# First norm of a two-layer diffusion block: row tiles are loaded first, scaled by the root and turned, then modulated by feature in four units

## The chip, the cores and the metric

The kernel runs on one core of a Trainium2 chip. The metric is the time of one execution on the device in microseconds, median of several runs. The program is written out by hand for each engine: TensorE (PE), VectorE (DVE), ScalarE (ACT), GpSimd (POOL) and SyncE (SP), which issues most of the transfers. The engines meet through semaphores alone.

## What is computed

Two layers work on 512 latent rows and 256 context rows of 1024 features. A layer norms its input and modulates it with a shift and a scale that come from a conditioning vector (one for the latent rows, another for the context rows), multiplies by an input projection, runs two kinds of attention, merges them, and goes on to a gated convolutional channel mixer, normed and modulated the same way. The change touches only the first norm and what feeds it. Cut to that:

```python
def rms_norm(x, g):
    xf = x.astype(jnp.float32)
    y = xf * lax.rsqrt(jnp.mean(xf * xf, axis=-1, keepdims=True) + EPS)
    return (y * g.astype(jnp.float32)).astype(x.dtype)

def modulate(x, g, shift, scale):
    return rms_norm(x, g) * (1 + scale) + shift

sc, scc = jax.nn.silu(c), jax.nn.silu(c_ctx)
# layer 0; ada_w is 1024 x 6144
mod_lat = jnp.split(sc @ ada_w[0] + ada_b[0], 6, axis=-1)
mod_ctx = jnp.split(scc @ ada_w[0] + ada_b[0], 6, axis=-1)
h_lat = modulate(x, pre_mix_g[0], mod_lat[0], mod_lat[1])
h_ctx = modulate(ctx, pre_mix_g[0], mod_ctx[0], mod_ctx[1])
p_lat, p_ctx = h_lat @ even_w_in[0], h_ctx @ even_w_in[0]   # 1024 x 1184
```

## The kernel before

The rows are six tiles of 128 (`NT` = 6, of which `LT` = 4 latent), the features eight chunks of 128 (`KC` = 8). Every large product is made of three matmuls, high by high, high by low and low by high (lines 888 to 890), so each activation and each weight is split: ScalarE writes the high part (`act_hi`, `w_hi`), VectorE subtracts it from the full value (`act_lo`, `w_lo`; line 1897).

The start has three stages. First the *wide* products: `silu(c)` for both streams times the first 2048 columns of `ada_w` (shift and scale), in four units of 512 columns (`wide_mm`, line 914), each unit loaded in two halves of 1 MB by SP (`wide_unit`, line 751). VectorE adds the bias (line 2390). Two matmuls per unit with the selector `sel` spread each result row over the 128 partitions (`wide_spread`, line 925); ScalarE copies the shifts out (line 1871), VectorE makes 1 + scale times gain (line 2397). Then the norm of each row tile: load (line 661), square on ScalarE (line 1525), root on GpSimd (lines 2438 and 2440), scale (line 1982) and shift (line 1987) on VectorE over 1024 features, eight transposes on TensorE (line 945), high part and low part out of PSUM (lines 1543 and 1897). Behind each tile's transposes TensorE makes the last tile's first half of chunk 0 of the input projection (`first_tile`: 416 columns, features 0 to 511, weight unit 0). When all six are through, it makes the second half with weight unit 1.

Then come chunks 1 (512 columns, units 2 and 3) and 2 (256 columns, units 4 and 5). Woven in by the table `ADA_AT` are the *early* products, the other 16 units of 256 columns of `ada_w` (`ada_mm`, line 903), on PSUM banks 6 and 7 in turn: `ring_free(r)` makes TensorE wait until round r - 2 has been read out. The first two stand behind the last tile of chunk 0, the third behind tile 1 of unit 2:

```python
ADA_AT = {(1, 5): [0, 1], (2, 1): [2], (2, 3): [3], (2, 5): [4], (3, 1): [5], (3, 3): [6], (3, 5): [7],
```

VectorE reads them out in `early_evac` (line 1910, four additions), which it reaches in program order only after the six tiles of chunk 0. For each of those six, ScalarE squares two parts (line 1634) and copies the tile (line 1642), GpSimd makes two roots (lines 2438, 2440), VectorE scales by them (line 2097), and GpSimd issues a store (line 2516). ScalarE may be at most two tiles ahead of GpSimd. Ahead of tile 0 ScalarE splits weight unit 2 (line 1509) and VectorE makes its low part. Constants for later are loaded from ScalarE's queue, three behind each row tile (line 1557), and VectorE waits for all of them (`const_in`) ahead of its split of unit 2.

Of the kernel before, what the change touches and what calls it, by code (L numbers as in the profile page):

```python
# [29 lines left out]
WIDES = 2 * D // WIDE  # L30
TZ_W = 2 * GRID_W - 1
# [126 lines left out]
def build(nc, I, C, out):  # L158
# [16 lines left out]
    with ctx:  # L175
# [19 lines left out]
        cvec, cexp = sb("cvec", [P, KC, 2]), sb("cexp", [P, KC, 2])  # L195
# [26 lines left out]
        def kilo(n):  # L222
# [5 lines left out]
        wide_row = arena[:, 8 * D:10 * D]  # L228
        wide_raw = [arena[:, 14 * D + n * KC * WIDE:14 * D + (n + 1) * KC * WIDE].rearrange("p (k c) -> p k c", k=KC)
                    for n in range(2)]  # L230
        wide_raw += [nc.alloc_sbuf_tensor_at(f"wide_raw{n}", [P, KC, WIDE], fp32, offset=act_at + n * 4 * KC * ROWS)
                     for n in range(2)]
        sel = sb("sel", [P, 2, P])
# [50 lines left out]
        pe_raw, x_first = pt[1][1], pt[1][0]  # L284
# [25 lines left out]
        wide_clear, wide_bias, ident_in = sem("wide_clear"), sem("wide_bias"), sem("ident_in")  # L310
        spread, shift_out = sem("spread"), sem("shift_out")
# [48 lines left out]
        CVEC = [(cvec[:, :, :], C["streams"])]  # L360
        FIRST = [(ident[:, :], C["ident"]), (sel[:, :, :], C["sel"])]
# [19 lines left out]
        def norm_growth(tiles, y, h, streams):  # L381
            return dict(t=2 * tiles * h, th=2 * tiles * h, y=tiles * y, h=tiles * h, xl=tiles, xs=tiles * y,
                        mod=streams * (y + 2 * h), gain=y + h, nm=1)
# [4 lines left out]
            ("ada", dict(t=WIDES)),  # L388
            ("norm0", dict(norm_growth(NT, 0, 1, 2), mod=0)),
# [16 lines left out]
        BASE, total = {}, dict.fromkeys("t th mm w ev st s tt pv hd y h xl xs mod gain nm nsq f g".split(), 0)  # L406
# [74 lines left out]
        def ada_round(layer, g):  # L481

            if layer == 0:
                return base("in0", "t") + ADA_IN0[g - ADA_FIRST]
            return base("up0", "t") + g

# [90 lines left out]
        def _(sp):  # L577
# [67 lines left out]
            def x_moves(name, tiles):  # L645
# [3 lines left out]
                for t in tiles:  # L649
# [3 lines left out]
                    if t >= 2 and NORMS[name][0] is None:  # L653
                        sp.wait_ge(h_scaled, base(name, "h") + t - 1)
                    elif t >= 2:
# [16 lines left out]
            def head_loads(name, a, before, weights=()):  # L672
# [26 lines left out]
                def load(p, s):  # L699
# [4 lines left out]
                    if a.name == "mla":  # L704
                        pe_q = x_first if p == 0 else x_raw[s].rearrange("p (t c) -> p t c", t=NT)
# [41 lines left out]
            def wide_unit(n):  # L747

                v = I["ada_w"][0].rearrange("(k p) c -> p k c", p=P)[:, :, n * WIDE:(n + 1) * WIDE]
                for half, (a, b) in enumerate(((0, KC // 2), (KC // 2, KC))):  # L750
                    sp.dma_start(wide_raw[n][:, a:b, :], v[:, a:b, :]).then_inc(wide_in[n][half], 16)

            wide_unit(0)
            sp.wait_ge(wide_clear, 1)
            sp.dma_start(wide_row[0:2, :], I["ada_b"][0:1, 0:2 * D].to_broadcast([2, 2 * D])).then_inc(wide_bias, 16)
            for n in range(1, WIDES - 1):
                wide_unit(n)
            gain_loads("norm0")
            wide_unit(WIDES - 1)
            x_moves("norm0", range(2))  # L760
            for n in range(2):
                k_unit(n, I["even_w_in"][0], 4 * n, 4, 0, MLA_IN)
            x_moves("norm0", range(2, NT))
# [5 lines left out]
            sp.wait_ge(t_free, WIDES)  # L769
# [4 lines left out]
            sp.wait_ge(h_ready, base("norm0", "h") + NT)  # L774
# [108 lines left out]
        def _(pe):  # L883
# [23 lines left out]
            def wide_mm(n):  # L907

                ring_free(n)
                for k in range(KC):  # L910
                    c = k % GROUPS * GROUP
                    if k % (KC // 2) == 0:
                        pe.wait_ge(wide_in[n][k // (KC // 2)], 16)
                    last = mm(bank(6 + n % 2, WIDE)[c:c + GROUP, :], silu[:, k, :], wide_raw[n][:, k, :],
# [3 lines left out]
            def wide_spread(n):  # L918

                pe.wait_ge(t_free, n + 1)  # L920
# [1746 lines left out]
```

## Time and profile before

| what | value |
|---|---|
| median of 3 runs | 1719.76 us (1718.31 to 1721.81) |
| profiled execution, its own time | 1721.04 us |
| profiled execution, span | 1719.3 us |
| PE busy | 1656.8 us, 96% |
| DVE busy | 1005.9 us, 59% |
| ACT busy | 624.3 us, 36% |
| POOL busy | 259.6 us, 15% |
| DMA | 211.34 MB, mean 123 GB/s |

The own time is the device time of the profiled execution; the span runs from its first to its last recorded instruction. Busy shares are means over stages with different limits: in the first 21 us the transfers are full and TensorE has pauses, later TensorE is nearly always busy. Matmuls overlap and their ends are modelled, so the distance from start to start is the better measure of one.

### The profile page before, as it was taken

To read this page: it belongs to the slowest core of one execution; us is meant where nothing else is said; L and a number is where in the kernel's file an instruction comes from. 1 tells how busy PE (TensorE), PEld (TensorE's weight loads), DVE (VectorE), ACT (ScalarE), POOL (GpSimd) and SP (SyncE) were. 2 spreads that over 40 slices of the span, in tenths; PEclk is the share of its full clock that TensorE was granted. 3 is DMA by queue.
4 is the path that set the end of the run, shared out by engine and by line. 5 is a ranking of instruction groups with operands and counts; after the bars stand their busy time and mean duration, and the time that the engine had idled before them with its cause. 6 is when DMAs were issued, how large, how long until landed. Compare 5 with 4: busy or idle time off the path is not lost.

```text
span 1719.3 us, 26521 instructions
## 1 busy us (share of the span) xinstructions
PE 1656.8 (96%) x9828; PEld 1334.2 (78%) x9828; DVE 1005.9 (59%) x1911; ACT 624.3 (36%) x1077; POOL 259.6 (15%) x420
## 2 busy tenths in 40 slices
PE   6999899999999999999999989998999999999998
PEld 2877566668898888888878878886678888888886
DVE  3666566764747777767776487215753744443445
ACT  3414555653321212121324434225543433323343
POOL 1413233331300000000000034204420300000000
PEclk9999999999999999999999999999999999999999
DMA  8586331286513353434334454323404443332243
GB/s 317 181 275 217 88 95 30 47 92 208 185 50 98 98 147 98 137 108 126 114 105 147 132 173 149 125 81 70 120 16 135 123 122 98 95 95 66 86 135 135
DMA packets 242582, 211.34 MB, mean 123 GB/s; under 512 B 54200, under 2 KB 204600, under 8 KB 242488
## 3 DMA queue, kind: packets, MB, share of 16 engines
q1 hardware_dynamic: 236186, 199.28, 39.3%
q0 software_dynamic: 4288, 9.10, 1.4%
q10 hardware_dynamic: 2016, 1.73, 0.4%
q8 instruction: 59, 0.97, 0.2%
q14 instruction: 33, 0.27, 0.1%
HBM read 186.58 MB, written 23.48 MB: 122 GB/s over the span
## 4 chain that ended last, share of the span: by engine, by line
PE 84%; DVE 4%; ACT 3%; POOL 3%; DMA 3%; issue 2%; SPq 1%; ACTq 0%; DVEq 0%
PE ps L1360 31%; PE ps L888 9%; PE ps L889 9%; PE ps L890 9%; PE ps L1125 4%; PE ps L1236 4%; PE ps L1031 3%; PE ps L1183 3%; PE ps L1370 2%; PE ps L1174 1%; PE ps L1344 1%; PE ps L1346 1%; PE ps L1345 1%; ACT arena L1721 1%; PE ps L945 1%
## 5 line engine op out<-in xcount | busy, mean ns | idle before, releaser
L1897 DVE TENSOR_TENSOR w_lo<-w_raw,w_hi 128x2048 fp32r<-128x2048 f32 (+3 forms) x112 | 204.0, 1822 | 244.3 <-ACT w_hi L1509 243.6
L888 PE MATMUL ps<-w_hi,act_hi 128*128 128x512 f32 (+2 forms) x872 | 337.9, 388 | 3.1 <-DVE act_lo L1897 2.0
L889 PE MATMUL ps<-w_lo,act_hi 128*128 128x512 f32 (+2 forms) x872 | 333.5, 382 | 0.0
L890 PE MATMUL ps<-w_hi,act_lo 128*128 128x512 f32 (+2 forms) x872 | 333.4, 382 | 0.0
L1360 PE MATMUL ps<-act_lo,w_hi 128*128 128x512 f32 (+1 forms) x912 | 278.1, 359 | 0.0
L1360 PE MATMUL ps<-act_hi,w_hi 128*128 128x512 f32 (+1 forms) x912 | 276.4, 357 | 0.0
L1360 PE MATMUL ps<-act_hi,w_lo 128*128 128x512 f32 (+1 forms) x912 | 274.4, 355 | 0.0
L1509 ACT ACTIVATE w_hi<-w_raw 128x2048 fp32r<-128x2048 f32 (+2 forms) x106 | 166.1, 1567 | 271.9 <-PE ps L890 208.3
L888 PEld LDWEIGHTS ps<-w_hi,act_hi 128*128 128x128 f32 x872 | 164.3, 188 | 40.1 <-issue 9.9
L890 PEld LDWEIGHTS ps<-w_hi,act_lo 128*128 128x128 f32 x872 | 164.3, 188 | 30.7
L889 PEld LDWEIGHTS ps<-w_lo,act_hi 128*128 128x128 f32 x872 | 164.5, 189 | 29.2
L1360 PEld LDWEIGHTS ps<-act_hi,w_lo 128*128 128x128 f32 x912 | 151.4, 189 | 27.6
L1360 PEld LDWEIGHTS ps<-act_hi,w_hi 128*128 128x128 f32 x912 | 149.1, 188 | 28.7 <-issue 3.8
L1360 PEld LDWEIGHTS ps<-act_lo,w_hi 128*128 128x128 f32 x912 | 150.4, 188 | 24.7
L1805 ACT ACTIVATE arena<-ps,conv 128x768 f32<-128x768 f32 (+1 forms) x44 | 39.0, 885 | 309.5 <-PE ps L1360 286.3
L2580 POOL TENSOR_SCALAR arena<-arena,rinv 128x256 f32<-128x256 f32 (+3 forms) x144 | 105.1, 730 | 262.0 <-DVE rinv L2221 262.0
L1953 DVE SCALAR_TENSOR_TENSOR arena<-arena,silu 128x256 f32<-128x256 f32 x336 | 137.3, 481 | 0.9
L1125 PE MATMUL ps<-ident,arena 128*128 128x128 f32 x730 | 118.6, 288 | 12.3 <-ACT arena L1704 7.5
L1125 PEld LDWEIGHTS ps<-ident,arena 128*128 128x128 f32 x730 | 79.7, 143 | 56.2 <-issue 29.7
L1721 ACT ACTIVATE arena<-arena,nb 128x768 f32<-128x768 f32 (+5 forms) x144 | 108.5, 754 | 19.6 <-DVE nb L2216 19.0
L2294 DVE SCALAR_TENSOR_TENSOR arena<-ps,conv,arena 128x511 f32<-128x511 f32 x66 | 41.6, 658 | 124.0 <-ACT arena L1805 124.0
L1704 ACT ACTIVATE arena<-ps 128x384 f32<-128x384 f32 (+2 forms) x163 | 67.4, 413 | 118.7 <-PE ps L1125 116.3
(155 smaller groups left out, 2112.1 us busy)
## 6 DMA issues: line engine op xcount, KB each, us to landing
arena<-in_ada_w SPq DMA_DIRECT2D x44, 1024.0 KB, 8.4
w_raw<-in_ffn_up SPq DMA_DIRECT2D x88, 512.0 KB, 5.2
w_raw<-in_ffn_down SPq DMA_DIRECT2D x88, 256.0 KB, 3.0
w_raw<-in_odd_w_in SPq DMA_DIRECT2D x20, 512.0 KB, 4.5
arena<-mods SPq DMA_DIRECT2D x16, 512.0 KB, 7.3
x_after_mix<-arena SPq DMA_DIRECT2D x10, 512.0 KB, 3.0
arena<-x_after_mix SPq DMA_DIRECT2D x10, 512.0 KB, 5.2
wide_raw<-in_ada_w SPq DMA_DIRECT2D x4, 1024.0 KB, 14.0
```

Of the source, the lines that this page charges most:

```text
L888: mm(out_, s_hi, m_hi, start=start, stop=False)
L889: mm(out_, s_hi, m_lo, start=False, stop=False)
L890: return mm(out_, s_lo, m_hi, start=False, stop=stop)
L1125: last = nc.tensor.transpose(bank(b)[:, n * P:(n + 1) * P], src, ident[:, :])
L1236: last = mm(o[:, t * P:(t + 1) * P], w, pt[k % 2][x][:, c, :], start=c == 0, stop=c == len(keys) - 1)
L1360: last = mm(o, wt[:, k, :], m[:, k, rows], start=st, stop=sp_)
L1509: A(w_hi[:, s, 0:n], w_raw[:, s, 0:n], ACT.Copy).then_inc(w_hi_done, 1)
L1704: A(dst, bank(6, n * P), ACT.Copy).then_inc(left_free, 1)
L1721: A(dst, src, ACT.Exp, bias=nb[:, s, x:x + 1], scale=-1.0, accum_out=rsum[:, s, x:x + 1])\
L1897: V.tensor_sub(out_, full, hi.bitcast(fp32)).then_inc(sem_, 1)
L1953: ins = V.scalar_tensor_tensor(out=ada_sum[:, v, :], in0=w, scalar=x, in1=ada_sum[:, v, :], op0=ALU.mult, op1=ALU.add)
L2580: Q.tensor_scalar(v, v, rinv[:, k % 2, x:x + 1], 1.0, ALU.mult, ALU.mult).then_inc(p_scaled, 1)
```

## The change

Row tiles now come first: SP loads all six before any weight. VectorE multiplies a tile by its root only (`normed`), TensorE turns it, and ScalarE copies the turned values, with features on the partitions, into `x_turned`. The modulation then is one number per partition for each chunk of features and each stream. The wide units are cut another way: unit n holds 256 columns of shift and the same 256 of scale, so that it completes features 256n to 256n + 255, two chunks. Per unit, TensorE makes the wide product, VectorE copies the rows out, TensorE turns them into columns (`wide_turn`, four matmuls with two columns), VectorE adds bias and makes (1 + scale) times gain. VectorE writes the full modulated values (`first_full`), ScalarE the high parts straight from `x_turned`, and VectorE the low parts, first for the latent rows, then for the context rows. TensorE's products of chunk 0 follow by unit, latent and context apart. The order of everything from chunk 1 on stays. The bias, the gain and both conditioning vectors now come in one packed constant; `sel` shrinks to two columns.

```diff
+    def wide_unit(n):                      # SP
+            for part in range(2):
+                src = v[:, a:b, part * D + n * FEATS:part * D + (n + 1) * FEATS]
+                sp.dma_start(wide_raw[n][:, a:b, part * FEATS:(part + 1) * FEATS], src)\
+                    .then_inc(wide_in[n][half], 16)
+    for t in range(NT):
+        first_rows(t)
+    wide_unit(0)
+    k_unit(0, I["even_w_in"][0], 0, 4, 0, MLA_IN)
+    wide_unit(1)
+    sp.wait_ge(t_done, 2 * NT)
+    wide_unit(2)
+    k_unit(1, I["even_w_in"][0], 4, 4, 0, MLA_IN)
+    sp.wait_ge(t_done, row_round(0) + 1)
+    wide_unit(3)
...
-    sp.wait_ge(t_free, WIDES)
+    sp.wait_ge(t_done, row_round(1) + 1)
     for i in range(2):
         early_unit(i)
     for n in (2, 3):
         k_unit(n, *units[n])
-    sp.wait_ge(h_ready, base("norm0", "h") + NT)
+    sp.wait_ge(first_lo, 2 * WIDES)
     early_unit(2)
...
+    def wide_turn(n):                      # TensorE
+        r = row_round(n) + 1
+        pe.wait_ge(t_free, r)
+        for c in range(WIDE // P):
+            last = mm(bank(6 + r % 2, 2, 2 * c), wide_row[:, c * P:(c + 1) * P], sel[:, :], start=True, stop=True)
+        last.then_inc(t_done, 1)
+    def products(n, tiles, part):
+        weights(n // 2)
+        pe.wait_ge(first_lo, part)
+        for t in tiles:
+            for j in range(FEAT_K):
+                last = three(bank(t, MLA_IN), act_hi[:, k, rows], act_lo[:, k, rows],
+                             w_hi[:, n // 2, cols], w_lo[:, n // 2, cols], k == 0, k == KC - 1)
+    for t in range(NT):
+        rows_turn(t)
+    wide_mm(0)
+    wide_turn(0)
+    products(0, latent, 1)
+    wide_mm(1)
+    products(0, context, 2)
+    wide_turn(1)
+    wide_mm(2)
+    products(1, latent, 3)
+    wide_turn(2)
+    products(1, context, 4)
+    wide_mm(3)
+    products(2, latent, 5)
+    wide_turn(3)
+    products(2, context, 6)
+    products(3, latent, 7)
+    products(3, context, 8)
+    for i in ADA_AT[1, NT - 1]:
+        ada_mm(i)
...
+    for t in range(NT):                    # ScalarE; square(0) and square(1) stand ahead
+        if t + 2 < NT:
+            square(t + 2)
+        turned(t)
+    for n in range(WIDES):
+        if n % 2 == 0:
+            w_loaded(n // 2)
+            split_hi(n // 2, n // 2, 4 * MLA_IN)
+        for v in range(2):
+            hi(n, v)
+        if n:
+            for dst, src in CONSTS[5 * (n - 1):5 * n]:
+                act.dma_start(dst, src, allow_slow_non_contiguous=True).then_inc(const_in, 16)
...
+    for t in range(NT):                    # VectorE
+        normed(t)
+    for n in range(WIDES):
+        modulation_columns(n)
+        modulated(n, 0)
+        if n == 0:
+            split_lo(0, 0, 4 * MLA_IN)
+        low(n, 0)
+        modulated(n, 1)
+        low(n, 1)
+        if n == 1:
+            split_lo(1, 1, 4 * MLA_IN)
```

The order of instructions moves as follows. On TensorE before, behind the last wide product stand the spreads and then the turns of the first row tile (`arena` is the working memory, here `wide_row` and the row tiles; `ps` is PSUM; the moving operand is named first, the stationary one second; `x3` are three alike):

```order
L925 MATMUL ps<-arena,sel 128x512 [waits t_free]
L925 MATMUL ps<-arena,sel 128x512
L925 MATMUL ps<-arena,sel 128x512 [waits shift_out,t_free]
L925 MATMUL ps<-arena,sel 128x512 [waits shift_out]
L945 MATMUL ps<-ident,arena 128x128 [waits t_free,h_ready]
L945 MATMUL ps<-ident,arena 128x128 x3
L945 MATMUL ps<-ident,arena 128x128 [waits t_free]
L945 MATMUL ps<-ident,arena 128x128 x3
```

Behind these come the first products, with the turns of the later tiles between them. On TensorE of the change, all turns are done by then, and behind them stands unit 0:

```order
L964 MATMUL ps<-ident,arena 128x128 [waits t_free]
L964 MATMUL ps<-ident,arena 128x128 x3
L935 MATMUL ps<-arena,silu 32x512 [waits wide_in00,t_free]
L935 MATMUL ps<-arena,silu 32x512 x3
L935 MATMUL ps<-arena,silu 32x512 [waits wide_in01]
L935 MATMUL ps<-arena,silu 32x512 x3
L944 MATMUL ps<-sel,arena 128x2 [waits t_free]
L944 MATMUL ps<-sel,arena 128x2 x3
L908 MATMUL ps<-w_hi,act_hi 128x416 [waits first_lo,w_lo_done]
L909 MATMUL ps<-w_lo,act_hi 128x416
L910 MATMUL ps<-w_hi,act_lo 128x416
```

The spreads over 512 columns are gone and the small turn has come in; the first product now waits for VectorE's `first_lo`, and between the products of unit 0 and the next ones stands the next wide product. On VectorE before, between the wide results and the first products:

```order
L2397 SCALAR_TENSOR_TENSOR arena<-ps,arena 128x512 [waits spread,gain_in]
L2397 SCALAR_TENSOR_TENSOR arena<-ps,arena 128x512 [waits spread] x3
L1982 SCALAR_TENSOR_TENSOR arena<-arena,rsx 128x1024 [waits rs_x,dve_self,shift_out]
L1987 TENSOR_TENSOR arena<-arena 128x1024 [waits h_scaled]
L1982 SCALAR_TENSOR_TENSOR arena<-arena,rsx 128x1024 [waits rs_x]
L1897 TENSOR_TENSOR act_lo<-ps,act_hi 128x4x128 [waits t_hi] x2
L1987 TENSOR_TENSOR arena<-arena 128x1024 [waits h_scaled]
L1897 TENSOR_TENSOR w_lo<-w_raw,w_hi 128x1664 [waits w_hi_done]
```

Each row tile took a scaling and a shift over 1024 features. On VectorE of the change, `rsx` are the roots:

```order
L2022 TENSOR_SCALAR arena<-arena,rsx 128x1024 [waits rs_x] x6
L2027 COPY arena<-ps 128x512 [waits t_done]
L2030 TENSOR_TENSOR first_mod<-ps,first_cols 128x8 [waits t_done]
L2033 SCALAR_TENSOR_TENSOR first_mod<-first_mod,first_cols 128x4 [waits t_free]
L2042 TENSOR_SCALAR first_full<-arena,first_mod 128x512 [waits first_mods]
L2042 TENSOR_SCALAR first_full<-arena,first_mod 128x512
L1953 TENSOR_TENSOR w_lo<-w_raw,w_hi 128x1664 [waits w_hi_done]
L1953 TENSOR_TENSOR act_lo<-first_full,act_hi 128x2x512 [waits first_hi,dve_self]
L2042 TENSOR_SCALAR first_full<-arena,first_mod 128x256 [waits first_mods]
L2042 TENSOR_SCALAR first_full<-arena,first_mod 128x256
L1953 TENSOR_TENSOR act_lo<-first_full,act_hi 128x2x256 [waits first_hi,dve_self]
```

What moved: a tile takes one TENSOR_SCALAR of 1024; the modulation is four short TENSOR_SCALAR per unit, and the low parts come from `first_full` in SBUF instead of PSUM. On ScalarE of the change, at units 1 and 2, the constants' loads stand ahead of the split of weight unit 1:

```order
L1571 ACTIVATE act_hi<-arena,first_mod 128x512 [waits first_mods,t_free]
L1571 ACTIVATE act_hi<-arena,first_mod 128x512
L1571 ACTIVATE act_hi<-arena,first_mod 128x256 x2
L1590 DMA band<-in_band 128x1152
L1590 DMA colmask<-in_colmask 128x96
L1590 DMA rope<-in_rope 128x128
L1590 DMA rope<-in_rope 128x256
L1590 DMA rope<-in_rope 128x512
L1546 ACTIVATE w_hi<-w_raw 128x1664 [waits w_in1]
L1571 ACTIVATE act_hi<-arena,first_mod 128x512 [waits first_mods,t_free]
L1571 ACTIVATE act_hi<-arena,first_mod 128x512
```

Before, both weight units were split ahead of all row tiles' high parts, and the constants went out two or three at a time.

## Rows read from the trace of the kernel before

**Rows 1.** The page of the kernel before, its first line.
```profile
span 1719.3 us, 26521 instructions
```

**Rows 2.** Windows, core 0: length, busy time per engine, granted clock, DMA share, GB/s.
```profile
3.00:21.00 18.00, 11.76 (x42) 2.26 (x46) 2.37 (x8) 0.90 (x3) 0.00 (x0) 1.00 1.05 389
...
35.00:45.00 10.00, 7.00 (x25) 6.17 (x26) 8.76 (x10) 5.08 (x9) 3.60 (x4) 0.50 0.75 225
...
62.00:85.00 23.00, 22.88 (x138) 20.24 (x136) 11.54 (x35) 10.44 (x32) 14.30 (x30) 1.00 0.40 126
85.00:158.00 73.00, 72.75 (x551) 57.65 (x552) 48.92 (x111) 15.55 (x29) 16.55 (x31) 1.00 0.77 251
99.00:101.00 2.00, 2.00 (x22) 1.26 (x15) 0.87 (x3) 0.82 (x1) 0.00 (x0) 1.00 1.02 354
```

**Rows 3.** Timeline of PE, 77 to 86 us: start, duration, what.
```profile
77.28 1.93 PE L903 MATMUL ps<-arena,silu 128*32 128x256 f32 x32
79.14 0.50 PE L888 MATMUL ps<-w_hi,act_hi 128*128 128x512 f32 x1
...
85.23 1.07 PE L903 MATMUL ps<-arena,silu 128*32 128x256 f32 x16 [0.35 <-DVE late_row L1910]
```

**Rows 4.** Timeline of DVE, 66 to 86 us.
```profile
66.73 2.29 DVE L1897 TENSOR_TENSOR w_lo<-w_raw,w_hi 128x2048 fp32r<-128x2048 f32 x1 [4.13 <-ACT w_hi L1509]
...
82.62 0.88 DVE L2097 SCALAR_TENSOR_TENSOR arena<-arena,rsh,g_mla 128x256 f32<-128x256 f32 x2 [1.51 <-POOL rsh L2440]
...
83.85 1.33 DVE L1910 TENSOR_TENSOR late_row<-ps,late_row 2x256 f32<-2x256 f32 x3
```

**Rows 5.** Timeline of POOL, 67 to 78 us.
```profile
67.39 1.68 POOL L2438 TENSOR_SCALAR rsh<-ssh 128x1 f32<-128x1 f32 x1 [12.99 <-ACT arena L1634]
...
75.06 0.62 POOL L2516 DMA_DIRECT2D proj_even<-arena  x1
...
77.58 0.61 POOL L2516 DMA_DIRECT2D proj_even<-arena  x1
```

**Rows 6.** Timeline of ACT, 64 to 67 us.
```profile
64.78 1.92 ACT L1509 ACTIVATE w_hi<-w_raw 128x2048 fp32r<-128x2048 f32 x1 [4.91 <-DMA w_raw<-in_even_w_in]
66.60 0.36 ACT L1634 ACTIVATE arena<-ps 128x256 f32<-128x256 f32 x1
```

**Rows 7.** Groups by shape, ACT: count, busy us, mean ns of one, idle before.
```profile
L1525 ACT ACTIVATE arena<-arena 128x1024 f32<-128x1024 f32 x22 | 23.3, 1058 | 23.2 <-DVE arena L2021 19.0 <-DMA arena<-in_x 3.2 <-DMA arena<-in_ctx 0.9
...
L1696 ACT ACTIVATE w_hi<-w_raw 128x512 fp32r<-128x512 f32 x8 | 4.9, 616 | 0.0
```

**Rows 8.** Timeline of PE, 20 to 46 us.
```profile
20.81 1.99 PE L914 MATMUL ps<-wide_raw,silu 128*32 128x512 f32 x16
...
35.45 1.97 PE L945 MATMUL ps<-ident,arena 128*128 128x128 f32 x8 [3.44 <-DVE arena L1987]
39.97 1.97 PE L945 MATMUL ps<-ident,arena 128*128 128x128 f32 x8 [2.54 <-DVE arena L1987]
...
43.04 0.55 PE L888 MATMUL ps<-w_hi,act_hi 128*128 128x416 f32 x1
43.38 0.55 PE L889 MATMUL ps<-w_lo,act_hi 128*128 128x416 f32 x1
...
45.03 0.35 PE L888 MATMUL ps<-w_hi,act_hi 128*128 128x416 f32 x1
45.22 0.35 PE L889 MATMUL ps<-w_lo,act_hi 128*128 128x416 f32 x1
```

**Rows 9.** Groups by shape, DVE.
```profile
L1897 DVE TENSOR_TENSOR act_lo<-ps,act_hi 128x512 fp32r<-128x512 f32 x48 | 31.1, 685 | 15.0 <-ACT act_hi L1543 14.5
...
L1897 DVE TENSOR_TENSOR act_lo<-arena,act_hi 128x1024 fp32r<-128x1024 f32 x22 | 26.7, 1219 | 4.2 <-ACT act_hi L1821 4.2
...
L1956 DVE TENSOR_SCALAR arena<-arena,silu 128x256 f32<-128x256 f32 x48 | 14.8, 351 | 0.7
...
L1897 DVE TENSOR_TENSOR w_lo<-w_raw,w_hi 128x1664 fp32r<-128x1664 f32 x2 | 3.8, 1884 | 0.0
```

More of the change, by code:

```diff
@@ L227, in build @@
         h_tok = [kilo(10), kilo(11), kilo(14)]
[L228 to L233, printed above, removed]
+        x_turned = arena[:, 0:KC * ROWS].rearrange("p (k r) -> p k r", k=KC)
+        x_first = [kilo(6 + t) for t in range(NT)]
+        wide_row = arena[:, 22 * D:22 * D + WIDE]
+        wide_raw = [arena[:, n * D:(n + 4) * D].rearrange("p (k c) -> p k c", k=KC) for n in (14, 18, 10, 14)]
+        first_full = nc.alloc_sbuf_tensor_at("first_full", [P, KC, ROWS], fp32, offset=act_at + 4 * KC * ROWS)
+        first_scrap = nc.alloc_sbuf_tensor_at("first_scrap", [P, 2, D], fp32, offset=act_at + 4 * (KC * ROWS + 5 * ROWS))
+        sel = sb("sel", [P, 2])
         at = [arena_at]
@@ L405, in build @@
         ]
-        BASE, total = {}, dict.fromkeys("t th mm w ev st s tt pv hd y h xl xs mod gain nm nsq f g".split(), 0)
+        BASE, total = {}, dict.fromkeys("t th mm w ev st s tt pv hd y h hs xl xs mod gain nm nsq f g".split(), 0)
         for name, growth in PHASES:
@@ L1866, in feed_down @@
                     step(0, 0, 1, n)
-            for b in range(4):
-                act.wait_ge(spread, b + 1)
-                n, v = b // 2, b % 2
-                A(mod_row[2][v][:, n * WIDE:(n + 1) * WIDE], bank(b, WIDE), ACT.Copy).then_inc(shift_out, 1)
-            norm("norm0")
+            first_norm()
             sizes = [4 * 512] * 2 + [4 * 256] * 2 + [2 * 8 * MLA_D, 16 * NOPE] + [2048] * 2
@@ new lines, in modulated @@
+                def modulated(n, v):
+                    dve.wait_ge(first_mods, n + 1)
+                    rows = (slice(0, LAT), slice(LAT, ROWS))[v]
+                    for j in range(FEAT_K):
+                        k = n * FEAT_K + j
+                        own.inc(V.tensor_scalar(first_full[:, k, rows], x_turned[:, k, rows],
+                                                first_mod[:, n, 1, j, v:v + 1], first_mod[:, n, 0, j, v:v + 1],
+                                                ALU.mult, ALU.add))
@@ new lines, in low @@
+                def low(n, v):
+                    own.wait()
+                    dve.wait_ge(first_hi, 2 * n + v + 1)
+                    rows = (slice(0, LAT), slice(LAT, ROWS))[v]
+                    chunks = slice(n * FEAT_K, (n + 1) * FEAT_K)
+                    minus_hi(act_lo[:, chunks, rows], first_full[:, chunks, rows], act_hi[:, chunks, rows],
+                             first_lo)
+                for t in range(NT):
[4 more added lines that the diff above has]
+                    if n == 0:
+                        split_lo(0, 0, 4 * MLA_IN)
+                    low(n, 0)
[3 more added lines that the diff above has]
+                        split_lo(1, 1, 4 * MLA_IN)
```

217 lines of the change are left out of this document (95 added, 122 removed).

## The prediction

> **What bounds the kernel now.** I read three kinds of view in this order: the stretches, to see which engine leaves no room where; the timelines of each engine around the places where TensorE stops; the groups by shape, for prices. The whole execution is 1719.3 us [rows 1]. The reader should see in the stretches [rows 2] that the edited part has two halves. Up to 21 us the DMA engines run without a pause at 389 GB/s, and TensorE's pieces follow the arrivals. From 62 to 85 us TensorE works 22.88 of 23 us, and from 85 to 158 us 72.75 of 73: there it is the bound, and a microsecond that TensorE loses stays lost. All of the edit lies ahead of 79 us, where TensorE begins the second chunk of the input projection (512 columns).
>
> The question is then what TensorE's start of that bound stretch hangs on. The TensorE rows there [rows 3] are: the two early products of the conditioning at 77.28 us, the second chunk at 79.14, two row tiles of it, and at 85.23 the third early product, `ada_mm(2)`. Its matmul has a wait of 0.35 us for VectorE's line 1910. That is `early_evac(0)`, which must free the PSUM bank (the ring of two, banks 6 and 7). So at 85.2 us two chains arrive together: TensorE's own, and the one that ends in `early_evac(0)`. Going back in the second: line 1910's last three of that product run from 83.85 to 85.18, close behind the last scaling of chunk 0 at 82.62 [rows 4]; that is paced by GpSimd's roots, whose store issues stand 2.52 us apart (75.06 and 77.58) [rows 5], six tiles long; the first root, at 67.39, took 1.68 us and ended only with VectorE's split of weight unit 2 (66.73 to 69.02) [rows 4, 5]; and that split waits for ScalarE's split of unit 2, which ends at 66.70, just as ScalarE squares the first tile at 66.60 [rows 6]. From the end of that split to the end of `early_evac(0)` is 85.18 - 69.02 = 16.2 us of work that the edit leaves as it is, in the same order. I call it the tail.
>
> **The change, part by part.** Everything is timed from the span's start; what I need is (a) when VectorE's split of unit 2 ends, which with 16.2 gives the earliest `ada_mm(2)`, and (b) when TensorE itself gets there.
>
> *Transfers.* Removed: the gain (0.5 MB) and the bias rows. Moved: six row tiles (3.1 MB) ahead of four units of `ada_w` (8.4 MB) and two of weights (1.7 MB), 13.2 MB in all. The wide units now have 1 KB rows instead of 2 KB. A stretch in which only such 1 KB rows moved shows 354 GB/s against 389 [rows 2], so I put the last wide unit between 13.2/0.389 + 3 = 37 us and 13.2/0.354 + 4 = 41 us. The two waits added on SP (all row tiles turned, first wide product done, both near 23 to 25 us by the sums below) come before its queue has drained, at about 25 us. TensorE wants the last unit at 54 us; transfers cost nothing, with 13 us of cover.
>
> *Row tiles.* Squares (1.06 us each plus an accumulator read, some 1.27) [rows 7] start at 5 us, the transposes when the identity is there, about 9.5. Eight transposes took 1.97 us at the lower clock [rows 8], six tiles 12 us, and with the ring of two banks between TensorE and ScalarE I come to 22.5 us (21 at the higher clock, 24 with every pause).
>
> *Unit 0.* The wide product takes 1.99 us warm [rows 8] and twice that cold: 2.9 between; to 25.4. VectorE copies 512 columns from PSUM, 0.69 [rows 9]: 26.1. The turn of the row into columns, four matmuls with 128x128 weights and 2 columns, is in no row; nearest are the eight transposes, 1.97 at the lower clock [rows 8] and half of that at the higher one: at least 0.5, at most 2, I take 1.1: 27.2. Two small vector operations, 0.4: 27.6. Then 2 modulations of 512, VectorE's split of weights 1.88, the low part 1.22 [rows 9]: with 0.48 for a modulation, 31.6.
>
> A modulation is a TENSOR_SCALAR between SBUF tiles. The nearest row is 351 ns for 256 columns, where a TENSOR_TENSOR of 512 from PSUM takes 685 [rows 9]; 0.48 to 0.69 for 512 are the bounds, and I take 0.48. At 0.69 the sum would hardly differ, because ScalarE makes the high part of the same columns beside it, 0.62 each [rows 7].
>
> *The products.* 144 matmuls of 416 columns, as before, 0.19 us apart warm (45.03 to 45.22) and 0.34 cold (43.04 to 43.38) [rows 8]. TensorE's order from 31.6: latent of unit 0, 24 matmuls, 4.55, plus 2.0 because TensorE has then been idle for 4 us and begins at the lower clock: 38.1; wide product 1, 2.0; context 2.3; turn 1.1: 43.5; wide product 2, 2.0: 45.5. VectorE and ScalarE need 2.9 from the turn (0.4, 1.25, 1.22), so the latent of unit 1 begins at 46.4 (0.9 of waiting); +4.55, turn 1.1, context 2.3, wide product 3 2.0: 56.3. Latent of unit 2 4.55, turn 1.1: 61.95. Context 2.3 hides most of the next 2.9: latent of unit 3 begins at 64.85. It ends at 69.4, the context at 71.7, the first two early products (1.93) [rows 3] at 73.6. Before, that was 79.14: TensorE arrives 5.5 us earlier.
>
> *(a).* From the fourth turn at 61.95: small ones 0.4, the high parts 1.25 and 0.85, ScalarE's split of unit 2 1.92 [rows 6], VectorE's 2.29 [rows 4]: 68.7. The first tile is complete at 64.85 + 1.13 = 66.0, in time. Before it was 69.02. So the head of the tail moves by -0.3 us only, and `early_evac(0)` ends at 84.9.
>
> *(b).* TensorE reaches `ada_mm(2)` at 73.6 + 5.35 (two tiles) = 78.95 and stands still for 5.9 us. The 5.5 us that it won are in that pause. What is late next is nothing new on the other engines: behind `early_evac(0)` they have the old order.
>
> *The pause has a price.* TensorE was idle up to 35.45 for 3.44 us [rows 8], and the stretch 35 to 45 us shows a granted clock of 0.50, its lower level (1.2 GHz); the matmuls from 43.04 run at 0.34 us, those from 45.03 at 0.19. Since the transposes began at 39.97 it was about 5 us of work at half speed, 2.5 us lost. That price falls now behind 84.9 us, where TensorE is the bound; nothing covers it. Bounds: 0 (the clock holds) and 3.
>
> The Trainium skill, "TensorE: Matmul & The Clock Gate", section "HAM oscillation — how this bites in real kernels", speaks against this change: idle gaps between matmul groups drop the engine to half clock, and each group then starts slow. The trace agrees for the gap ahead of 35.45. By that rule applied to the pauses between units as well the sum is rival B's.
>
> **Sum:** -0.3 + 2.5 = +2.2 us. The profiled execution took 1721.04 us with a span of 1719.3; by it 1723.2. The median of the three runs is 1719.76, 1.3 below the profiled one, and I carry the difference over: **1722.0 us**. A measurement of this kernel tells about 0.2%, 3.4 us, from no change (1716.3 to 1723.2).
>
> The Trainium skill, "VectorE: DVE Perf Modes", section on the perf-mode tier table, gives fp32 tensor_scalar between SBUF tiles two elements a cycle, tensor_tensor one. The 351 ns row fits it; by the one-a-cycle price each unit would be at most 0.4 us later, and the sum +3.
>
> **The rivals.**
> - *A, the forecast, 0.50:* head of the tail within 1.5 us of where it was, pause of 5 to 6 us, clock lost. 1719 to 1725; 0.38 of it inside 0.2%, 0.12 above.
> - *B, slower, 0.18:* the clock stays low through unit 0. Its place: wide product 0, the turn, latent 0, wide product 1, context 0, up to 45 us. For it: the engine is idle in four places between 27 and 47 us, and in the stretch of 35 to 45 us it was busy for 7.00 of 10 us and stayed at 0.50 [rows 2]. Against: from 31.6 TensorE's queue is full for 12 us. Half of 9 us more at the lower clock is 4.5: head of the tail at 73, 1726.5. It decides from 1.3 us on.
> - *C, 0.10:* ScalarE issues five constant loads in one go ahead of its split of unit 1, and VectorE's copy for the third unit stands behind its part of that split; if ScalarE stands for the issues (0.4 us each), the third turn comes 1.5 to 2 us late: 1723.5 to 1724. Half of it inside.
> - *D, 0.04:* transfers late after all (1 KB rows, and the constants beside them): last unit after 54 us, beyond 1725.
> - *E, 0.11:* all my middles are high: row tiles at 21, wide product warm, turns of 0.5. Head of the tail at 64.5; with the lost clock 1717.8, without it 1715.3.
> - *F, faster, 0.07:* the tail is shorter because six finished tiles come 1.1 us apart instead of 2.3, and TensorE doesn't stop. It keeps 5.5 us: 1714.3. Against: 2.52 us from store to store is GpSimd's own pace [rows 5], longer than a tile's 2.3 us of products, so faster tiles don't shorten it.
>
> **How the numbers follow.** Same: 0.38 + 0.05 (C) + 0.04 (E) = 0.47. Slower: 0.12 + 0.18 + 0.05 + 0.04 = 0.39. Faster: 0.07 (E) + 0.07 (F) = 0.14. For the range: B's 1726.5 with the 3 us bound of the clock goes to 1728; below, to 1716, inside E. 1716 to 1728 leaves out F, the end of E and part of D, 0.15 or so. A alone has 1719 to 1725.
>
> **What the profile after would show.** Right: second chunk at 73 to 75 us; a pause of TensorE of 5 to 6 us ahead of `ada_mm(2)`, released by VectorE's `early_evac`; line 1910's first group ending near 85; granted clock 0.5 for some microseconds around 85; the last wide unit landed by 42. Wrong, if `ada_mm(2)` doesn't wait (F), if the second chunk begins after 76 (B, C), if TensorE waits for `wide_raw` after 45 us (D), or if first products begin before 29 us (E). Least known are the turn's price, the clock through unit 0 and the start of the row tiles.

## The result, and the profile after

Over 20 executions each, the changed kernel took 1723.39 us (1720.55 to 1726.01) and the kernel before 1721.48 us in the median; the ratio is 1.0016 (95% interval 1.001 to 1.0022). One of the 20 executions of the kernel before took 4153.69 us and isn't in the ratio; without it that median is 1721.34 us. The changed kernel is slower by an amount that is clear of noise and whose middle lies inside the 0.2% called no change ahead of time. The profiled execution took 1724.28 us.

The page of the changed kernel, its first line (before: [rows 1]):
```profile
span 1722.6 us, 26591 instructions
```

The stretches, in the columns of [rows 2]:
```profile
3.00:21.00 18.00, 7.50 (x41) 6.22 (x42) 4.83 (x9) 10.74 (x22) 5.27 (x12) 1.00 1.05 374
35.00:45.00 10.00, 9.56 (x66) 6.25 (x64) 2.20 (x6) 1.80 (x3) 0.30 (x1) 1.00 0.89 276
62.00:85.00 23.00, 16.48 (x103) 13.56 (x101) 14.57 (x40) 12.95 (x36) 14.11 (x30) 0.94 0.24 74
85.00:158.00 73.00, 72.78 (x538) 57.32 (x542) 48.21 (x109) 15.56 (x29) 16.55 (x31) 0.97 0.75 242
82.00:86.00 4.00, 0.78 (x8) 0.40 (x12) 3.19 (x8) 0.00 (x0) 2.15 (x4) 0.54 0.04 8
86.00:89.00 3.00, 3.00 (x17) 1.73 (x10) 2.93 (x4) 0.00 (x0) 0.54 (x2) 0.50 0.89 283
89.00:92.00 3.00, 3.00 (x14) 2.49 (x13) 1.73 (x5) 0.00 (x0) 0.00 (x0) 0.97 1.08 347
```

Between 62 and 85 us TensorE now works 16.48 of 23 us instead of 22.88, and it comes out of that stretch at half clock: the granted clock is 0.54 from 82 to 86 us, 0.50 to 89, and 0.97 behind that. The same stretch of 35 to 45 us that was all at 0.50 before is at 1.00.

TensorE's timeline, in the part that answers to [rows 3] and a little on:
```profile
72.31 1.93 PE L923 MATMUL ps<-arena,silu 128*32 128x256 f32 x32
74.18 0.50 PE L908 MATMUL ps<-w_hi,act_hi 128*128 128x512 f32 x1
...
85.22 1.94 PE L923 MATMUL ps<-arena,silu 128*32 128x256 f32 x16 [5.30 <-DVE late_row L1966]
87.09 0.80 PE L908 MATMUL ps<-w_hi,act_hi 128*128 128x512 f32 x1
87.68 0.63 PE L909 MATMUL ps<-w_lo,act_hi 128*128 128x512 f32 x1
88.11 0.63 PE L910 MATMUL ps<-w_hi,act_lo 128*128 128x512 f32 x1
...
93.74 1.07 PE L923 MATMUL ps<-arena,silu 128*32 128x256 f32 x16
```

The early products stand at 72.31 us (77.28 before), the second chunk at 74.18 (79.14 before), and `ada_mm(2)` at 85.22 (85.23 before), now with 5.30 us of idle time ahead of it, put down to VectorE's `early_evac`. That product takes 1.94 us instead of 1.07, and the matmuls behind it stand 0.43 us apart (87.68 to 88.11) where they stand 0.23 apart at the full clock.

The other chain answers to [rows 4 to 6]. Its part on VectorE, from the timeline:
```profile
66.70 2.29 DVE L1953 TENSOR_TENSOR w_lo<-w_raw,w_hi 128x2048 fp32r<-128x2048 f32 x1
...
82.61 0.87 DVE L2183 SCALAR_TENSOR_TENSOR arena<-arena,rsh,g_mla 128x256 f32<-128x256 f32 x2 [1.51 <-POOL rsh L2504]
...
83.83 1.33 DVE L1966 TENSOR_TENSOR late_row<-ps,late_row 2x256 f32<-2x256 f32 x3
```
On GpSimd, the first root and two store issues:
```profile
67.57 1.47 POOL L2502 TENSOR_SCALAR rsh<-ssh 128x1 f32<-128x1 f32 x1 [26.31 <-ACT arena L1694]
...
75.04 0.62 POOL L2580 DMA_DIRECT2D proj_even<-arena  x1
...
77.56 0.61 POOL L2580 DMA_DIRECT2D proj_even<-arena  x1
```
And on ScalarE, the last high parts, the split of weight unit 2 and the first square:
```profile
62.35 0.82 ACT L1571 ACTIVATE act_hi<-arena,first_mod 128x512 fp32r<-128x512 f32 x1 [7.57 <-DVE first_mod L2033]
...
64.76 1.90 ACT L1546 ACTIVATE w_hi<-w_raw 128x2048 fp32r<-128x2048 f32 x1
66.75 0.39 ACT L1694 ACTIVATE arena<-ps 128x256 f32<-128x256 f32 x1
```

The tail is where it was. The split of weight unit 2 ends at 68.99 us (69.02 before), the stores stand 2.52 us apart, and the last piece of `early_evac(0)` ends at 85.16 (85.18 before). So the two traces show the forecast's picture: 5 us won at the head, 5.3 us of standing still, then a lower clock.

Lined up instruction by instruction from the end, ScalarE's instructions of the changed kernel lie 1.8 us behind those of the kernel before from 90 to 173 us. Then 1.6 us of it are gone at once, 0.1 to 0.3 us is left up to 985 us, and by the end of the spans it is 3.3. This is what the experiments had to settle first: is the 1.8 us taken up again at 174 us by the attention's first steps, and what is lost behind 985?

### The profile page after: what moved, and what is told of

Its sections match the earlier page's. It is cut to its first block, busy times and chain, and to the rows that moved or that the text cites. A ratio compares the mean times of both kernels' runs of the same rounds, so it can differ in the third digit from the quotient of the medians.

```text
span 1722.6 us, 26591 instructions
## 1 busy us (share of the span) xinstructions
PE 1651.2 (96%) x9844; PEld 1336.9 (78%) x9844; DVE 999.5 (58%) x1920; ACT 630.9 (37%) x1089; POOL 255.2 (15%) x420
## 4 chain that ended last, share of the span: by engine, by line
PE 85%; DVE 4%; ACT 4%; POOL 2%; issue 2%; DMA 2%; SPq 1%; ACTq 0%; DVEq 0%
PE ps L1403 31%; PE ps L908 10%; PE ps L909 10%; PE ps L910 10%; PE ps L1167 4%; PE ps L1279 4%; PE ps L1083 3%; PE ps L1226 3%; PE ps L1413 2%; PE ps L1217 1%; PE ps L964 1%; PE ps L1387 1%; PE ps L1389 1%; PE ps L1388 1%; ACT arena L1781 1%
## 5 line engine op out<-in xcount | busy, mean ns | idle before, releaser
L910 PEld LDWEIGHTS ps<-w_hi,act_lo 128*128 128x128 f32 x872 | 164.7, 189 | 31.3
```

What stands on the lines that cost most here:

```text
L910: return mm(out_, s_lo, m_hi, start=False, stop=stop)
```

## Experiments

The theory was: the tail of chunk 0 sets when the bank comes free, so TensorE stands ahead of `ada_mm(2)` for as long as the change brings it there early, and pays some 1.8 us of half clock behind that. The main rival was that the bound lies further back, in what comes behind the projection, so that neither the stop nor the clock counts.

**1. The third early product later.** In the changed kernel, one line of the table of places. It also moves the four early products behind the third by two tiles each:

```diff
-ADA_AT = {(1, 5): [0, 1], (2, 1): [2], (2, 3): [3], (2, 5): [4], (3, 1): [5], (3, 3): [6], (3, 5): [7],
+ADA_AT = {(1, 5): [0, 1], (2, 3): [2], (2, 5): [3], (3, 1): [4], (3, 3): [5], (3, 5): [6, 7],
```

> Kernel after, with the third early product (and the four behind it) two or three tiles later in TensorE's order, so that TensorE has four tiles of the second chunk to work on before it needs the bank that early_evac(0) frees. Theory (the fixed tail of the first chunk holds the early products, and the five microseconds by which the chunk starts earlier are spent in the pause ahead of ada_mm(2), plus 1.8 us of half clock behind it): no pause over 0.3 us and no half clock between 79 and 92 us; the second chunk's first unit ends about 7 us earlier than in the changed kernel (near 91 instead of 98), and the execution is 5 to 7 us shorter than the changed kernel's: ratio to before 0.997 (0.996 to 0.998). Rival 1 (what comes behind the projection, transfers or the first attention steps, sets the time, as it already swallowed the 1.8 us between 158 and 184 us): the pause goes, but the time stays within 1.5 us of the changed kernel's, 1722 to 1724. Rival 2 (the late early products hold back a weight unit's transfer in SyncE's order): TensorE stops for weights at unit 4 or later by 2 us or more.

It took 1715.15 us (1712.46 to 1716.99, six executions) against 1721.03 of the kernel before on the same chip, ratio 0.997 (0.9957 to 0.9982). In its waits of TensorE from 60 to 170 us, the columns being the sum in us, the times and the longest, `early_evac` is gone:
```profile
PE ps L908 <- DVE act_lo L1953: 1.4, 1, 1.4
PE ps L1167 <- ACT arena L1764: 1.1, 1, 1.1
PE ps L908 <- ACT arena L1715: 0.8, 1, 0.8
PE ps L1226 <- ACT arena L1773: 0.7, 1, 0.7
```
The stretches show full clock and no gap where the changed kernel had both:
```profile
82.00:86.00 4.00, 4.00 (x25) 2.99 (x26) 2.79 (x7) 0.00 (x0) 1.98 (x6) 1.00 0.04 8
86.00:89.00 3.00, 3.00 (x26) 2.09 (x19) 2.90 (x5) 0.00 (x0) 0.97 (x2) 1.00 0.73 215
85.00:158.00 73.00, 72.22 (x564) 56.62 (x563) 51.49 (x118) 19.73 (x39) 17.25 (x33) 1.00 0.86 268
```
Both rivals fall. No wait for weights appears, and the time moves in full: 7.9 us by the ratios (0.997 against 1.0016), 7.1 us by the traces (5.3 of stop and 1.8 of clock).

**2. The evacuations earlier.** TensorE's order untouched, VectorE's changed:

```diff
 def ada(u, b):
     if layer == 0:
-        for i in ADA_AT.get((u, b), []):
+        for i in ({(1, 2): [0], (1, 3): [1], (1, 5): []}.get((u, b), ADA_AT.get((u, b), []))):
             early_evac(i)
```

> Kernel after, with VectorE evacuating the first two early products behind the scaling of the third and fourth tile of chunk 0 rather than behind the sixth; TensorE's order is untouched. Theory: early_evac(0) ends near 78.5 us instead of 85.2, TensorE reaches ada_mm(2) at 79.9 and doesn't stop, no half clock there; time 5 to 7 us below the changed kernel's, ratio to before 0.997 (0.996 to 0.998), the same as in the run with the later product. Rival 1 (the time is set behind the projection): within 1.5 us of the changed kernel's. Rival 2 (the evacuations of 1.8 us each, set between the tiles, lengthen chunk 0's chain by as much, and the split of the third weight unit behind it): the split ends at 89 or later and TensorE stops there for weights; gain below 3 us.

1716.48 us (1713.33 to 1718.15), ratio 0.9976 (0.9967 to 0.9986); no wait for `early_evac` and no half clock between 80 and 170 us. VectorE's split of the third weight unit starts at 84.44 us instead of 86.90, so rival 2 falls as well. The same stop is taken away from the other side, for a gain that can't be told from that of experiment 1.

**3. Both moves on the kernel before, one at a time.** The edit of 2 first:

> Kernel before, with the same move of the first two evacuations in VectorE's order. Theory: TensorE reached ada_mm(2) of the kernel before at 85 us, when the bank had just come free, so the move gives it nothing there: ratio to before 0.9995 to 1.001, ada_mm(2) still at 85.0 to 85.3. Rival (the order in VectorE's queue was bad by itself, whatever the change): it gains 2 us or more here too.

1719.73 us (1716.7 to 1721.48) against 1721.03, ratio 0.9995 (0.9986 to 1.0005). `ada_mm(2)` is at 84.17 us rather than at 85.0 to 85.3, since this trace's early products stand 0.65 us earlier (76.63 against 77.28) and the wait of 0.35 us is gone. Then the edit of 1:

> Kernel before, with the early products' places moved as in the run with the later product. Theory: TensorE reached ada_mm(2) there at 85 us, 0.4 us before the bank came free, so the move can give at most 0.4 us: ratio 0.999 to 1.0005, and the 5.9 us that the same move gave on the changed kernel against the kernel before are those of the change. Rival (the early products' places were bad in both): 2 us or more here too.

1721.42 us (1718.82 to 1723.21) against 1721.01, ratio 1.0002 (0.9993 to 1.0011). Neither move can be told from nothing here. The second is the less clean of the two tests: its trace has a new wait of 1.26 us for `early_evac` at a transpose at 123.67 us, which the changed kernel with the same move doesn't have. The first has no new wait for `early_evac`. So the gain of the first two experiments isn't a flaw that both kernels had in equal measure: it is what the change brings to TensorE and the old places spend.

**4. Kept busy through the stop.** In the changed kernel, before `ada_mm(2)`:

```diff
+if (u, b) == (2, 1):
+    bank_free(2)
+    for _ in range(23):
+        mm(bank(2, 512), act_hi[:, 0, 2 * P:3 * P], w_hi[:, 0, 0:512], start=True, stop=True)
 for i in ADA_AT.get((u, b), []):
     ada_mm(i)
```

> Kernel after, with 23 products of 512 columns that nobody reads in TensorE's queue ahead of ada_mm(2) (into the bank that the next tile overwrites), so that it works through the pause of 5.3 us. Theory: no half clock at ada_mm(2), which takes 1.07 us rather than 1.94; ada_mm(3) starts at 91.9 to 92.1, as in the kernel before (91.99), instead of 93.74, so the 1.8 us are the clock's and not the pause's. If the 1.8 us count in the time, ratio to before 1.000; if they are taken up again by the stretch at 170 to 186 us, as between the two traces, the time stays at the changed kernel's, 1.0015, and the half clock that the kernel before shows at 174.6 us shows again. Rival (the loss behind the pause is contention and not the clock): ada_mm(2) takes 1.9 us all the same.

1721.86 us (1719.27 to 1723.48), ratio 1.0008 (0.9999 to 1.0017): 1.5 us under the changed kernel's two medians (1723.39, and 1723.37 below), 1.2 by the ratios. `ada_mm(2)` takes 1.07 us again, `ada_mm(3)` follows 6.69 us behind it (92.50 - 85.81) instead of 8.52, the clock stands at 1.00 from 82 to 89 us, and at 140 us ScalarE's instructions lie 1.24 us ahead of those in the changed kernel's trace although the first chunk ended 0.6 us later, which makes 1.8. In the trace the lower clock is the whole loss behind the stop, and contention none of it. The time agrees but doesn't prove it: the interval holds the ratio of the changed kernel, 1.0014 to 1.0016, as well as 1.

**5. The changed kernel once more.**

> The changed kernel as it is, once more. Theory: the stop ahead of ada_mm(2) (5.3 us) and the half clock from about 82 to 89 us are of the kernel and stand here again, with ada_mm(3) 1.7 to 1.9 us later than in the kernel before; ratio 1.0010 to 1.0022. The stretches at half clock after 950 us that were in the changed kernel's first trace and not in the one of before (near 1021 us and 6.8 us near 1229) are of the execution: in the five other traces so far there was none near 1229; none is expected here. Rival (they are of the changed kernel): 6.8 us of half clock again near 1229, and the time at 1224.

1723.37 us (1720.46 to 1725.82) against 1721.01, ratio 1.0014 (1.0005 to 1.0023). Its span was 1718.8 us, shorter than that of the kernel before, in an execution of the same code. Its timeline of TensorE shows the stop again, to a hundredth, and `ada_mm(3)` follows 8.41 us behind (93.44), so that 1.65 us are lost behind the stop. It stands 1.45 us later than in the kernel before (91.99), less than expected, in part since this trace's head is 0.2 us earlier:
```profile
85.03 1.94 PE L923 MATMUL ps<-arena,silu 128*32 128x256 f32 x16 [5.30 <-DVE late_row L1966]
```
This ended two wrong readings of the first pair of traces. A stretch of 6.8 us at half clock near 1229 us, and one of 3.4 near 1021, stood in the changed kernel's first trace; in the second neither stands, so they are of the execution and explain no difference between the kernels. In the second trace ScalarE's last instructions lie 0.5 us ahead of those of the kernel before. And the 1.6 us that seemed to be taken up again at 174 us were a stretch of half clock in the one trace of the kernel before. Its window, in the columns of [rows 2]:
```profile
174.00:178.00 4.00, 3.48 (x12) 1.80 (x16) 0.00 (x0) 0.37 (x1) 0.00 (x0) 0.58 0.95 174
```
That of the kernel before with the later product (experiment 3), whose code is the same there:
```profile
174.00:178.00 4.00, 2.87 (x21) 1.30 (x19) 0.22 (x1) 0.87 (x2) 0.00 (x0) 1.00 1.04 229
```
0.58 in one, 1.00 in the other; and ScalarE's lag in this trace to the one of the kernel before shrinks by the same 1.6 us at that place (from 0.66 us behind to 0.98 ahead). So nothing in these traces points to a place behind the projection that absorbs the loss. One stretch stays open: 3.4 us at half clock that begin between 1348 and 1356 us, worth 1.5 us, stand in the nine traces without the long stop ahead of `ada_mm(2)`, that of the kernel before among them, and in none of the three traces that have it (both of the changed kernel, and experiment 7's first). Whether it belongs to the execution or to the kernel no run here settles.

**6. Both moves together.**

> Kernel after with both moves, the later product and the earlier evacuations. Theory: each alone took the whole stop away, so both together give no more than the better one: 1714.5 to 1716.5, ratio 0.9962 to 0.9978. Rival (the early products' chain behind the first two was still paced by the evacuations at 83.8 to 87.3 us, and a bank comes free late again): 1 us or more less than with the later product alone, below 1714.

1715.57 us (1714.11 to 1717.15), ratio 0.9971 (0.9961 to 0.998). As expected, each alone took away all that was to be had.

**7. A shorter tail.** One `pow` over both roots of a row tile, in GpSimd's part of chunk 0:

```diff
+if layer == 0:
+    for k, w in enumerate((Q_RANK, KV_RANK)):
+        own.inc(Q.tensor_scalar(rsh[:, nsq % 2, k:k + 1], ssh[:, nsq % 2, k:k + 1],
+                                1.0 / w, EPS, ALU.mult, ALU.add))
+    own.wait()
+    two = rsh[:, nsq % 2, 0:2]
+    Q.tensor_tensor(two, two, mhalf[:, 0:2], ALU.pow).then_inc(head_rs, 1)
+    return
```

> Kernel after with a shorter tail: in chunk 0 GpSimd takes both roots of a row tile with one pow over two columns instead of two pows over one (TENSOR_SCALAR, TENSOR_SCALAR, pow, rather than each pow behind its own TENSOR_SCALAR); TensorE's, ScalarE's and VectorE's orders are those of the changed kernel. Per tile it takes away one pow of 0.55 us and about 0.1 us of hand-over, of 2.52 us. Theory (the tail of six tiles, paced by these roots, sets when the bank comes free): early_evac(0) ends 3 to 4.5 us earlier, at 80.7 to 82.2; TensorE stops 0.8 to 2.3 us ahead of ada_mm(2) instead of 5.3, the half clock there goes or halves, and the execution is 3 to 6 us shorter than the changed kernel's: 1717.5 to 1720.5, ratio 0.998 to 0.9995. Rival 1 (the tail is paced by the evacuations on ScalarE or by VectorE's scaling, and the roots only fill its gaps): early_evac(0) ends within 1 us of 85.2 and the time stays 1722 to 1724. Rival 2 (the stop shrinks, but the half clock comes all the same and comes elsewhere): 1720.5 to 1722.

1719.62 us (1718.43 to 1720.29), ratio 0.9998 (0.9989 to 1.0006), from a change of GpSimd alone. The median is 3.8 us under the changed kernel's, but this chip is another one, on which the kernel before took 1719.77 us rather than 1721.01 and 1721.03; by the ratios (0.9998 against 1.0014 to 1.0016) it is 2.8 to 3.1 us. GpSimd's timeline, two roots of a tile and two store issues:
```profile
71.05 0.57 POOL L2566 TENSOR_SCALAR rsh<-ssh 128x1 f32<-128x1 f32 x2
71.70 0.69 POOL L2570 TENSOR_TENSOR rsh<-rsh,mhalf 128x2 f32<-128x2 f32 x1
...
76.98 0.61 POOL L2588 DMA_DIRECT2D proj_even<-arena  x1
...
79.00 0.60 POOL L2588 DMA_DIRECT2D proj_even<-arena  x1
```
TensorE's timeline at `ada_mm(2)`:
```profile
83.64 1.93 PE L923 MATMUL ps<-arena,silu 128*32 128x256 f32 x16 [2.83 <-DVE late_row L1966]
```
Two TENSOR_SCALARs one behind the other and a pow over two columns take 0.57 and 0.69 us. The stores stand 2.02 us apart rather than 2.52, and the stop is 2.83 us rather than 5.30. The stop's end came 2.5 us earlier against the head of the same trace (which lay 0.9 us later than the changed kernel's), less than the 3 to 4.5 that I expected: 0.50 us a tile instead of 0.65, since a pow over two columns takes longer than one over one, and over the five tiles behind the first. The half clock stayed, half as long (83.4 to 86.8 us by the granted clock, against 82.3 to 89.2), but nearly all of it fell on work, where in the changed kernel 2.9 us of it fell into the stop. `ada_mm(2)` takes 1.93 us, and `ada_mm(3)` follows 8.15 us behind it, against 8.52 in the changed kernel and 6.76 in the kernel before, so 1.4 us are lost rather than 1.8. Rival 1 falls: the roots do pace the tail. Rival 2 came true in part: the stop shrank and most of the clock's loss stayed; the ratio lies above the 0.998 to 0.9995 of the theory. The same with the product later:

> The later product and the one pow in one kernel. Theory: with the product later, TensorE no longer waits for anything that the tail gates, so a tail that is 3 to 4.5 us shorter buys nothing more: 1714.5 to 1716.5, within 1 us of the later product's 1715.15 (1715.57 with both moves). Rival (the tail also holds what comes behind: the split of the third weight unit on VectorE, the transfers that the evacuations release, the stores of the latents): 1.5 us or more below, under 1714.

1715.34 us (1712.27 to 1719.67), ratio 0.9973 (0.9962 to 0.9983). (Its profiled execution had two more stretches at half clock and a span of 1718.0.) With the stop gone a gain from the shorter tail can't be told from nothing. The three lengths of the stop, each with its clock, are 5.3 + 1.8 = 7.1 us, 2.8 + 1.4 = 4.2 and 0. By the ratios, each to the kernel before on its own chip (1.0014 to 1.0016, 0.9998, and 0.997 to 0.9973), the first two lie 7.1 to 7.9 and 4.3 to 4.8 us above the last, which is the same within the intervals.

**8. The load order undone**, with the later product so that the head shows in the time:

```diff
+wide_unit(0)
 for t in range(NT):
     first_rows(t)
-wide_unit(0)
```

> Kernel after with the later product, and the transfers of the first modulation unit issued ahead of the row tiles rather than behind them. It undoes the load order of the change alone. Theory: with the stop gone, the beginning of the kernel counts in the time in full; the turning of the row tiles, which is queued ahead of wide_mm(0) in TensorE's order, then starts later by the time of these transfers (2 MB; the traces show about 300 to 330 GB/s where the transfers are dense, so 6 to 7 us, less the 4 us or so for which TensorE and VectorE had slack with each other), and the second chunk's start moves from 74.5 to 77 to 81 us: time 2.5 to 6.5 us over that of the later product, 1717.5 to 1721.5. Rival 1 (the transfers of the later units and weights set the beginning, and their sum is unchanged): within 1 us of the later product's. Rival 2 (the beginning is hidden by the tail even now): within 1 us too, but with the second chunk starting later and the stop gone.

1719.15 us (1715.7 to 1722.48), ratio 0.999 (0.9981 to 0.9999): 4.0 us over the later product. Its timeline of TensorE, with the first transposes and the second chunk's early products:
```profile
14.87 3.81 PE L964 MATMUL ps<-ident,arena 128*128 128x128 f32 x16 [8.65 <-DVE arena L2022]
...
75.19 1.93 PE L923 MATMUL ps<-arena,silu 128*32 128x256 f32 x32
```
The first transposes are at 14.87 us, 2.9 later than in the changed kernel (11.97), and the early products at 75.19 instead of 72.31, 2.9 later too (2.4 against the later product's own trace, 72.8): nothing in between makes it up. The medians say 4.0 us, the ratios 3.4 (0.999 against 0.997), with some 2 us of uncertainty on such a difference. Both rivals fall, and the row tiles' place in the load order is worth 2.4 to 4 us, once the time can see it. VectorE's first scaling moved by more, from 8.04 us (in the later product's trace) to 13.97; the 2 MB are 5.6 us at the 376 GB/s of the stretch from 3 to 21 us, for which I had taken 300 to 330. With the row tiles first this scaling ends about 3.4 us before TensorE's first transposes at 12.15 us, which by the profile wait for the small constant `sel` (5.95 us of idle time). Whether an earlier load of that constant would win part of these 3.4 us was not tried.

## Why the prediction was right, and where its sums were off

**What bounds the kernel, and the tail.** Right. The length from the end of the split to the end of `early_evac(0)` was to stay 16.2 us, and it is 85.16 - 68.99 = 16.17. That it is what TensorE waits for is shown twice, by taking the wait away at either end (1 and 2), and that GpSimd's roots pace it by shortening them (7).

**The head of the tail** was to move by -0.3 us and moved by -0.03. The fourth turn ended at 61.54 us (61.95 forecast), but VectorE's two short instructions with their hand-overs took 0.8 us to the first high part instead of 0.4, and the four high parts 2.4 us instead of 2.1. I gave ScalarE 0.62 us for a high part of 512 columns, by a plain copy [rows 7]. It took more:
```profile
43.20 0.82 ACT L1571 ACTIVATE act_hi<-arena,first_mod 128x512 fp32r<-128x512 f32 x1 [13.43 <-DVE first_mod L2033]
...
44.63 0.59 ACT L1571 ACTIVATE act_hi<-arena,first_mod 128x256 fp32r<-128x256 f32 x1
```
0.82 and 0.59 us for 512 and 256 columns, against 0.62 and 0.42 or so forecast. Here ScalarE reads its scale and its bias from columns of their own, and the groups by shape of the kernel before had nearer rows, one with the bias from a column (`nb`), one with scale and bias from columns (`conv`):
```profile
L1721 ACT ACTIVATE arena<-arena,nb 128x512 f32<-128x512 f32 x32 | 23.0, 718 | 3.7 <-DVE nb L2216 3.6
...
L1805 ACT ACTIVATE arena<-ps,conv 128x512 f32<-128x512 f32 x22 | 17.1, 778 | 80.3 <-PE ps L1360 73.4 <-issue 5.2 <-PE ps L1370 0.9
```
616 ns plain, 718 with one such column and 778 with two: the nearest row would have given 0.78 instead of 0.62. That the columns are the cause is read from these rows; no run changes them alone. The low parts wait for them on VectorE, and TensorE stands 1.64 us ahead of unit 1 (0.9 forecast) and 1.44 us ahead of unit 3, where the sum has 0.6 (64.25 to 64.85):
```profile
22.99 1.92 PE L935 MATMUL ps<-arena,silu 128*32 128x512 f32 x16 [0.25 <-ACT arena L1562]
25.72 1.05 PE L944 MATMUL ps<-sel,arena 128*128 128x2 f32 x8 [0.81 <-DVE arena L2027]
31.30 0.69 PE L908 MATMUL ps<-w_hi,act_hi 128*128 128x416 f32 x1 [4.52 <-DVE act_lo L1953]
...
46.20 0.42 PE L908 MATMUL ps<-w_hi,act_hi 128*128 128x416 f32 x1 [1.64 <-DVE act_lo L1953]
...
65.35 0.42 PE L908 MATMUL ps<-w_hi,act_hi 128*128 128x416 f32 x1 [1.44 <-DVE act_lo L1953]
```
Against that, the first products started at 31.30 us (31.6 forecast), the turn of a row took 1.05 us (1.1 forecast), and the modulation of 512 columns 0.50 us (0.48): VectorE's 1.00 for two of them. TensorE arrives 5.0 us earlier instead of 5.5.

**The pause** of 5.9 us is 5.30. The second chunk began at 74.18 us instead of 73.6; its two tiles kept TensorE for 5.7 us (74.18 to 79.92) where I took 5.35 from [rows 3], which leaves out the end of the last product; and the bank came 0.3 us later than the 84.9 forecast.

**The clock** was to cost 2.5 us and cost 1.8. The row of before that I took it from had the engine at half speed for about 5 us of work. Here the half clock began at about 82.3 us, while TensorE was still standing (0.54 over 82 to 86 us is 0.3 us at full clock and 3.7 at half), and ended at about 89.2: 4 us of work at half speed, of which some 2 are lost. Nearly half of the granted stretch fell where nothing ran. The Trainium skill, "TensorE: Matmul & The Clock Gate", section "HAM oscillation — how this bites in real kernels", warns of this cost of an idle gap between groups of matmuls; the trace agrees, with 1.94 us for a product that takes 1.07. By experiment 4 it is 1.2 to 1.5 us of time, within the noise of that comparison.

**The sum** was +2.2 us, and the two comparisons give 1.9 and 2.4 us between medians (ratios 1.0016 and 1.0014). The forecast of 1722.0 us is 1.4 under the measured 1723.39, because the median of the first three executions of the kernel before (1719.76) that it was tied to was itself 1.7 under that of twenty. That the sum comes out so close is in part luck: the head of the tail was taken 0.3 us too early and the clock 0.7 us too dear, and with the terms as the traces show them it is 1.8 us. Whether the remaining 0.1 to 1 us are noise or a cost that isn't in the sum stays open.

**The rivals.** B (half clock through unit 0): the granted clock is 1.00 from 35 to 45 us, and the half clock of this part lies from 27 to 35; it ended 3 us into the products of unit 0. C: ScalarE's queue issued the five constants beside its high parts (43.30 to 45.58), and the split of unit 1 began at 45.63, without a gap. D: TensorE waited for no wide unit; the transfers of the last one were in by 39 us. E: first products at 31.3, not before 29. F: TensorE did stop.

**What the prediction did not say** is the larger thing: that the microseconds stood there to be had. It priced the pause and found it full; the change with one line more is 0.9970 of the kernel before, and neither piece alone is faster than it.

## What to carry to other kernels

When a change brings one engine early to a place where it already met another chain, look at once for what keeps it there: here it was the place of one small product in the order, and moving it (with those behind it) by two tiles turned 2 us lost into 5 to 6 us won. A stop ahead of a stretch that TensorE bounds costs its length and, on top, the half clock behind it (1.4 to 1.8 us in the traces here). Take a second trace of the same kernel before you explain a difference far from the edit: two traces of equal code differed by 3.8 us of span.

## What the runs showed of the hardware that I had not expected

- Beside the half clock that follows the stop, every trace has more of it further on, and two traces of the same kernel differ in where: 6.8 us near 1229 and 3.4 near 1021 stand in one and not in the other. A stretch of 3.4 us shifted all that follows by 1.5 to 1.6 us (at 174 and 1355 us).
- A shorter stop cost nearly the same clock: 1.4 us were lost behind 2.8 us of standing still, 1.65 and 1.8 behind 5.3.
- GpSimd's pow over two columns takes 0.7 us, over one 0.55: two single ones cost 0.4 us more than one double.
